# Forgetting attention's projections as seven products of quarters in place of eight, in a stage of eight heads

## The reference

```python
h = _rmsnorm(x, norm_w) * (1.0 + scale[:, None, :]) + shift[:, None, :]
proj = jnp.einsum("bsd,de->bse", h, w_in)
z_ssm, xbc, dt_raw, q, k, v, z_att, f_logit, g_logit = jnp.split(proj, offsets, axis=-1)
...
    logits = jnp.einsum("bhqd,bhkd->bhqk", qi, k).astype(jnp.float32) * scale
    logits = logits + fi[..., :, None] - f_cum[..., None, :]
    logits = jnp.where(pi[:, None] >= kpos[None, :], logits, -jnp.inf)
    probs = jax.nn.softmax(logits, axis=-1).astype(v.dtype)
    return jnp.einsum("bhqk,bhkd->bhqd", probs, v)
...
return o * jax.nn.silu(z)
```

## Time and profile before

| | us |
|---|---|
| median of 3 runs | 2056.05 |
| lowest and highest | 2053.98 to 2056.51 |
| the profiled execution | 2053.39 |
| its span, first to last instruction | 2051.7 |
| stage 5's eight heads in it | 626 to 1153 |

### The profile page before, as it was taken

The page is one execution under the profiler, slowest core; times in us unless marked ns, Lnnn a source line. Parts: engine busy times, 40 slices in busy tenths (PEclk is TensorE's granted clock), DMA queues, the critical chain, the costliest instruction groups (busy, mean ns, idle before and its releaser), DMA issues. The chain is left out here.

```text
span 2051.7 us, 26009 instructions
## 1 busy us (share of the span) xinstructions
PE 1942.3 (95%) x9700; PEld 1565.9 (76%) x9700; DVE 992.7 (48%) x1217; ACT 770.7 (38%) x1143; POOL 161.0 (8%) x319
## 2 busy tenths in 40 slices
PE   6899999999999999999999999969999998999997
PEld 4678787777887887888878788747777877888786
DVE  5586444555322334333343344479343344655865
ACT  4423343244213443444343342243234345442422
POOL 1000110110100000000000010002100001110100
PEclk8899999999999999999999999989999999999998
DMA  8541655543531111111112343232411111211302
GB/s 269 204 64 41 103 96 110 103 139 118 155 101 31 41 41 51 31 41 41 41 31 61 123 147 99 82 112 77 120 45 44 33 31 41 63 31 36 124 29 92
DMA packets 165535, 166.35 MB, mean 81 GB/s; under 512 B 10594, under 2 KB 143130, under 8 KB 165210
## 3 DMA queue, kind: packets, MB, share of 16 engines
q1 hardware_dynamic: 151424, 116.01, 18.3%
q0 software_dynamic: 13760, 49.30, 10.8%
q10 hardware_dynamic: 282, 0.09, 0.0%
HBM read 132.22 MB, written 33.16 MB: 81 GB/s over the span
## 5 line engine op out<-in xcount | busy, mean ns | idle before, releaser
L288 PE MATMUL acc<-ha_hi,w_hi 128*128 128x512 f32 x1152 | 469.1, 407 | 5.6 <-ACT stash L301 4.4
L288 PE MATMUL acc<-ha_hi,w_lo 128*128 128x512 f32 x1152 | 452.1, 392 | 0.0
L288 PE MATMUL acc<-ha_lo,w_hi 128*128 128x512 f32 x1152 | 450.6, 391 | 0.0
L288 PEld LDWEIGHTS acc<-ha_hi,w_hi 128*128 128x128 f32 x1152 | 217.7, 189 | 50.5 <-issue 6.5
L288 PEld LDWEIGHTS acc<-ha_hi,w_lo 128*128 128x128 f32 x1152 | 217.0, 188 | 47.7
L288 PEld LDWEIGHTS acc<-ha_lo,w_hi 128*128 128x128 f32 x1152 | 217.8, 189 | 42.0
L257 DVE TENSOR_TENSOR w_lo<-w_raw,w_hi 128x1024 fp32r<-128x1024 f32 x128 | 157.6, 1231 | 159.1 <-ACT w_hi L253 156.0
L271 PE MATMUL acc<-ha_hi,w_hi 128*128 128x512 f32 x592 | 187.3, 398 | 28.1 <-DVE ha_lo L1801 13.5
L271 PE MATMUL acc<-ha_lo,w_hi 128*128 128x512 f32 x592 | 184.5, 393 | 0.0
L271 PE MATMUL acc<-ha_hi,w_lo 128*128 128x512 f32 x592 | 183.9, 392 | 0.0
L271 PEld LDWEIGHTS acc<-ha_hi,w_hi 128*128 128x128 f32 x592 | 110.3, 190 | 58.8 <-issue 15.7
(11 more groups left out here) (444 smaller groups left out, 2749.1 us busy)
## 6 DMA issues: line engine op xcount, KB each, us to landing
w_raw<-in_w_in SPq DMA_DIRECT2D x99, 512.0 KB, 3.9
acs_bc<-acs_scr POOLq DMA_DIRECT2D x8, 1024.0 KB, 16.0
w_raw<-in_w_out SPq DMA_DIRECT2D x11, 512.0 KB, 3.9
x_tok<-in_x SPq DMA_DIRECT2D x8, 512.0 KB, 7.3
w_scale<-in_w_ada SPq DMA_DIRECT2D x8, 512.0 KB, 9.6
w_shift<-in_w_ada SPq DMA_DIRECT2D x8, 512.0 KB, 8.9
xt_scr<-xt SPq DMA_DIRECT2D x1, 4096.0 KB, 18.2
w_ada_g<-in_w_ada SPq DMA_DIRECT2D x8, 512.0 KB, 10.1
```

The source lines that it names most:

```text
L288: mm = pe.matmul(acc[:, 0, half * HALF:(half + 1) * HALF], w[:, n % 2, k, :], x[:, k, half * HALF:(half + 1) * HALF], start=(k == 0 and i ...
```

## The change

A pair of weight tiles (q and k of a head; v and z; two gate tiles) times the activations is a product of a matrix of 2 x 2 quarters with one of 2 x 2 quarters: the two tiles, each cut into rows 0 to 511 and 512 to 1023, and h cut in the same rows and into two halves of the tokens. That takes eight products of quarters, each of 4 k x 3 passes = 12 matmuls. The new kernel uses Strassen's form (in the variant of Winograd), which takes seven, with sums of quarters as operands and sums of the products as results:

- `a11`, `a12`, `s2`, `s1`, `s3`, `s4`, `a22` name the seven weights of a pair, in the order in which they run. Two pairs make a head: products 0 to 6 and 7 to 13.
- The sums of weights are made by VectorE for each pair: `weight_sums` (two operations and drains) and `weight_sums_in_place` (two more). Each of the 14 operands of 128x512 is then split in its own: `product_hi` on ScalarE, `product_lo` on VectorE. They rotate through four slots in the same buffers, which is why a loop body has two heads (`odd`).
- The sums of the quarters of h (`t1`, `t2`, `t3`, `t4`) are made once, ahead of the loop, by VectorE, and split as well; they and the other new buffers lie where `ya_hi` and `ya_lo` were.
- The product's result is read from PSUM not by ScalarE alone: `keep` (ScalarE, four a head) and `read` (VectorE, ten a head, with an addition), and `add_kept5` adds once more.
- A head's high and low part of y go to memory (`y_hi_scr`, `y_lo_scr`) and are loaded into `ya_hi` and `ya_lo` in the last head, by four DMAs, three of which stage 6 waits for ahead of its first matmul (`rows`).
- The order of each engine in a head is written out line by line. `fox_fills` and the sharing by parts are gone.
- The semaphores count products now, so later waits on them are shifted by `counted`.

```diff
+        PRODUCTS_EXTRA = (14 - 4) * FOX_HEADS
+        def counted(n):
+            return n + (PRODUCTS_EXTRA if n >= N_MIX2 else 0)
...
+        def product_lo(dve, q, h, odd):
+            dve.wait_ge(hi_done, FIRST + q + 1 + PER_HEAD * h)
+            dve.tensor_tensor(product_slot(w_lo, q, odd), weight_of(q), product_slot(w_hi, q, odd).bitcast(F32), ALU.subtract
+                              ).then_inc(lo_done, 1)
+        def weight_sums(dve, pair, h):
+            a11, a21, a22 = w_raw[:, W0, K1, :], w_raw[:, W1, K1, :], w_raw[:, W1, K2, :]
+            dve.drain()
+            raw_landed(dve, 0, pair, h)
+            raw_landed(dve, 1, pair, h)
+            dve.tensor_tensor(a21, a11, a21, ALU.subtract)
+            dve.drain()
+            dve.tensor_tensor(w_sum[:, :, :], a22, a21, ALU.subtract)
+            dve.drain().then_inc(w_summed, 1)
...
         def sp_5(sp):
+            product_done(9)
+            sp.wait_ge(y_saved, Y_SAVED + 48 * last)
+            sp.dma_start(ya_hi[:, 0:4, :].bitcast(F32), y_hi_scr[:, 0:4, :]).then_inc(y_back, 16)
+            product_done(10)
+            sp.dma_start(ya_hi[:, 4:7, :].bitcast(F32), y_hi_scr[:, 4:7, :]).then_inc(y_back, 16)
+            for i in range(2):
+                load_w(sp, N_MIX2 + i, cols(io["w_proj_att"], i * P))
+            product_done(11)
+            sp.dma_start(ya_lo[:, 0:4, :].bitcast(F32), y_lo_scr[:, 0:4, :]).then_inc(y_back, 16)
+            sp.wait_ge(*read_count(12, last))
+            sp.wait_ge(late_saved[0], LATE_SAVED)
+            sp.dma_start(ya_lo[:, 4:7, :].bitcast(F32), y_lo_scr[:, 4:7, :]).then_inc(y_tail, 16)
+            save_late(2, 12)
+            save_late(3, 13)
...
         def pe_5(pe):
+                def fill(q):
+                    pe.wait_ge(lo_done, FIRST + q + 1 + PER_HEAD * h)
+                    pe.wait_ge(*read_count(q - 2, h))
...
+                    for k in range(KH):
+                        for i, (w, x) in enumerate(((w_h, hi), (w_h, lo), (w_l, hi))):
+                            mm = pe.matmul(bank(q), w[:, k, :], x[:, k, :], start=(k == 0 and i == 0),
+                                           stop=(k == KH - 1 and i == 2))
...
+                scores(0)
+                scores(1)
+                fill(0)
+                fill(1)
+                scores(2)
+                fill(2)
+                fill(3)
+                turn_probs(0)
+                fill(4)
+                weigh_values(0)
...
         def act_5(act):
+                keep(0)
+                hi(3)
+                exps(0)
...
+                copies(5)
+                copies(6)
+                exps(7)
+                keep(10)
+                copies(7)
...
         def dve_5(dve):
+            split_lo(dve, N_FOX + 1)
+            quad(quad_12, K1, T2)
+            quad(quad_11, K1, T1)
+            dve.tensor_tensor(quad_11[:, :, :], quad_12[:, :, :], quad_11[:, :, :], ALU.subtract)
+            quad(quad_22, K2, T2)
+            dve.tensor_tensor(quad_12[:, :, :], quad_22[:, :, :], quad_12[:, :, :], ALU.subtract)
+            split_lo(dve, N_FOX + 2)
+            dve.tensor_tensor(quad_22[:, :, :], quad_22[:, :, :], quad_11[:, :, :], ALU.subtract)
+            t_lo(1, t1_lo[:, :, :], quad_11[:, :, :], t1_hi[:, :, :])
+            quad(quad_21, K2, T1)
+            dve.tensor_tensor(quad_21[:, :, :], quad_21[:, :, :], quad_22[:, :, :], ALU.subtract)
+            t_lo(2, t3_lo[:, :, :], quad_12[:, :, :], t3_hi[:, :, :])
+            t_lo(3, t2_lo[:, :, :], quad_22[:, :, :], t2_hi[:, :, :])
+            split_lo(dve, N_FOX + 3)
...
+                normalise(7)
+                read(11)
+                gate(0)
+                add_kept5(1)
+                read(12)
...
+                    weight_sums(dve, 2, h)
+                    lo(14)
+                gate(1)
...
+                    lo(15)
+                    weight_sums_in_place(dve)
+                read(13)
```

More of the change, by code:

```diff
@@ new lines, in head @@
+                copies(0)
+                exps(2)
+                keep(3)
+                copies(1)
+                copies(2)
+                hi(7)
+                hi(8)
+                hi(9)
+                exps(3)
+                exps(4)
+                copies(3)
+                hi(10)
+                hi(11)
+                keep(7)
+                exps(5)
+                copies(4)
+                hi(12)
+                exps(6)
+                hi(13)
+                copies(5)
@@ L1520, in head @@
+                copies(6)
+                exps(7)
+                keep(10)
+                copies(7)
+                if last:
+                    split_hi(act, N_MIX2)
+                else:
+                    hi(14)
+                    hi(15)
                 act.wait_ge(y_gated, 2 * h + 4)
                 if last:
-                    act.wait_ge(late_saved[0], LATE_SAVED)
-                act.activation(row(ya_hi, h), y_head[:, :], ACT.Copy).then_inc(x_hi_done, 1)
-            with act.Fori(0, FOX_HEADS - 1) as h:
-                head(h)
@@ L1527, in act_5 @@
-            head(FOX_HEADS - 1, last=True)
+                    act.activation(ya_hi[:, FOX_HEADS - 1, :], y_head[:, :], ACT.Copy).then_inc(x_hi_done, 1)
+                else:
+                    act.wait_ge(y_saved, Y_SAVED + 48 * h)
+                    for i in range(2):
+                        e = act.activation(y_hi[i][:, :], y_head[:, i * HALF:(i + 1) * HALF], ACT.Copy)
+                    e.then_inc(x_hi_done, 1)
+                    hi(16)
+            with act.Fori(0, FOX_HEADS // 2 - 1) as j:
+                head(2 * j, 0)
+                head(2 * j + 1, 1)
@@ new lines, in head @@
+                lo(3)
+                read(1)
+                normalise(0)
+                lo(4)
+                read(2)
+                lo(5)
+                lo(6)
+                normalise(1)
+                logits(2)
+                read(4)
+                normalise(2)
+                add_kept5(0)
+                logits(3)
+                read(5)
+                weight_sums(dve, 1, h)
+                lo(7)
+                logits(4)
+                lo(8)
+                normalise(3)
@@ new lines, in head @@
+                read(6)
+                lo(9)
+                normalise(4)
+                weight_sums_in_place(dve)
+                logits(5)
+                read(8)
+                lo(10)
+                normalise(5)
+                logits(6)
+                lo(11)
+                read(9)
+                normalise(6)
+                logits(7)
+                dve.drain().then_inc(fbc_used, 1)
+                lo(12)
+                lo(13)
+                normalise(7)
+                read(11)
@@ L1586, in dve_5 @@
+            with dve.Fori(0, FOX_HEADS // 2 - 1) as j:
+                head(2 * j, 0)
+                head(2 * j + 1, 1)
+            head(FOX_HEADS - 2, 0)
+            head(FOX_HEADS - 1, 1, last=True)
             end_stage(dve, 5)
```

366 lines of the change are left out of this document (271 added, 95 removed).

## The result

| | us |
|---|---|
| before, median of 4 runs | 2056.28 (2053.98 to 2058.67) |
| after, median of 4 runs | 2004.02 (2003.16 to 2004.76) |
| ratio, 95% interval | 0.9746 (0.9729 to 0.9762) |
| profiled execution, before and after | 2053.39 and 2004.76 |

The change takes 52.3 us by the medians, where 40 were forecast. The rest of this text works with the 48.6, which can be followed in the two traces.

A forecast was written before the change was run, and what follows sets the result against it. TensorE at its pace was taken to bound stage 5. Loop 43.6 less, minus 2.5 ahead and 1 behind, gave 40.1 us less: 2053.4 to 2013.3 profiled, 2016.0 as median; 8-in-10 range 2008 to 2038.

The forecast's parts named there:

- The removed matmuls: In each head, 24 fewer matmuls at 0.227 us save 5.44 us, 43.5 us over eight heads.
- The waits of `weigh_values`: In the heads, TensorE's waits for ScalarE's copy of the turned probabilities go, saving 4.9 us in all.
- one more change of kind: In each head, one more change between fills and attention on TensorE costs about 0.1 us, 0.8 us in all.
- The allowance for missed slack: In the heads, some tight places delay TensorE: 0.5 us a head, 4 us in all.
- VectorE's load: In a head, VectorE's busy time rises by 20.1 us to 44.9; with mask waits 48.8 of 60, so it fits.
- the rival: In the heads, VectorE's slack is not enough and TensorE waits 2 to 4 us a head: 2036 us; chance 20%.
- The slow rival: In the heads, VectorE becomes the bound at 66.1 us a head: about 2061 us, slower; chance 7%.
- Ahead of the loop: Before the first head, sums of h's quarters delay tile +3's low part; TensorE waits, costing 2.5 us.
- A lower granted clock in stage 5: In the attention stage, a listed sign that the forecast is wrong; no size given.
- Behind the loop: After the last product, returning y and the later `gate6` load together cost 1 us (bounds -0.6 and +11).
- The delay that I feared from GpSimd: After the last product, `gate6` loads later; VectorE's work moves some 4 us, leaving N_MIX2+2's low part no slack.
- GpSimd's copies under VectorE: In a head, q's copies slow VectorE's low parts by at most 0.8 us, hidden; 6.4 us in eight heads if uncovered.

The follow-up runs named there:

- The changed order alone: Kernel before with the last three parts of the fills (t = 5, 6, 7) moved between `turn_probs` and `weigh_values`: 2045.87 us, ratio 0.9954.
- the two runs with more work on it: Changed kernel with low parts of a head's product weights computed twice on VectorE: all 14, 2044.95 us; seven, 2012.93 us.
- the kernel with +3 early: Changed kernel with VectorE making tile +3's low part ahead of those of `t3` and `t2`: 2001.95 us, ratio 0.9738.
- two products twice: Changed kernel with the matmuls of products 3 and 10 of each head done twice, 24 more a head: 2049.37 us, ratio 0.9973.
- 172 operations: Kernel before with four heads in the body of VectorE's loop (two turns): 2055.38 us, one run.
- 43 and 86 operations: Kernel before, with one head in VectorE's loop body (median 2056.28 us), and with two heads in it (2056.49 us, one run).

## Why the prediction was too high

The time lies 12 us below the forecast and 4 below the low end of the range. The ledger holds 8.5 of the 12. The other 3.5 say nothing of the kernel: the forecast added 2.7 us to come from the profiled execution to the median, and after the change the profiled one lies 0.7 above its median. By the steps of the prediction:

**The removed matmuls: right.** 5.44 us a head were forecast and 5.45 measured.

**The waits of `weigh_values`: the mechanism right, the size wrong, and the largest miss.** I took the 4.9 us of the wait row as the gain of something to do in that place. The changed order alone gave 9.35 us, and the changed kernel is 1.4 us a head, 11 us, shorter than its matmuls explain. Of this the changed order alone gave 1.15 us a head, and 1.08 are seen in the starts at t = 6 and 7. The row is right in who waits for whom, but its idle starts at a modelled end, and for the price of a gap one must compare starts: 1.28 us from `turn_probs` to `weigh_values`, where seven transposes at 0.11 take 0.8. Both starts are in the trace of before. I also charged 0.8 us for one more change of kind; no run prices it by itself. Where the last 0.3 us of the 1.4 a head come from was not separated: the written order differs in more places than these, and the products are read in another way.

**The allowance for missed slack: half right in size, wrong in kind.** I put down 4 us since eight places had 0.3 to 1.5 us of slack. None was missed: the steady heads have no wait at all. The loss was 2.6 us where 4 stood in the sum, and it came from two jumps of VectorE's loop, which I had not considered, as the trace of before has seven jumps without any. Together, 43.6 + 11.2 - 2.6 = 52.2 us, and the ledger has 51.6.

**VectorE's load: right, and the rival rightly not the likeliest.** 43.5 us busy for 44.9. I had found it idle 7.7 us a head; the two runs with more work on it put what can be used at some 4. The rival's price was right in kind: with 9.8 us more of work a steady head grows by 3.9 to 4.7 us. The slow rival, heads of 66 us with VectorE as the bound, was 7 us a head away; even with the 9.8 us more the heads without a jump took 63.8 at most.

**Ahead of the loop: the wait right, the cost short by its second half.** The wait ahead of +3 was to be 2.5 us and is 2.43, for the reason given. But in the 4.6 us behind it the granted clock is 0.63, and pairs of matmuls start 0.85 us apart instead of 0.45: 1.9 us more, and none of it with the wait away. The upper bound of 4 was just passed (4.4). A lower granted clock in stage 5 was named as a sign of being wrong, and for this stretch it was one.

**Behind the loop: the transfer right, the price too high.** In the 20 us from 1086 on the DMA engines moved 333 GB/s and not 230. The transfers were to land 1.6 us behind the last product (the prediction's own numbers, 19.5 us for 6.8 million bytes and 2 to start, less 20.9, give 0.6); N_MIX2 starts 1.3 us behind it (1106.81 + 0.23 to 1108.37), released by them. So the wait of N_MIX2 for a DMA, named as a sign of being wrong, is there with 1.2 us, but shorter than the 2.1 us of before; and in the run with VectorE's loop written out ScalarE holds it for 1.0 us instead. Against before that is 0.9 us less, where 0.6 less was forecast for this part. The delay that I feared from GpSimd did happen: timelines of GpSimd and VectorE after, for the earlier trace rows,

```profile
1115.59 0.55 POOL L2020 DMA_DIRECT2D gate<-ga_scr  x1 [23.99 <-DMA ga_scr<-next_z]
```

```profile
1128.19 1.22 DVE L265 TENSOR_TENSOR w_lo<-w_raw,w_hi 128x1024 fp32r<-128x1024 f32 x1
```

`gate6` is loaded 7.2 us behind N_MIX2's start instead of 2.7. The low part that is queued behind it ends at 1129.4, needed at 1108.37 + 21.8 = 1130.2: 0.8 us of slack are left of 4, and no time is lost. So the term was -0.9 and not +1.

**GpSimd's copies under VectorE.** In the kernel with +3 early, the first sum of weights falls under them and takes 1.46 us instead of 0.69 (618.85 and 620.39 above), as the low part in the earlier trace rows took 2.07 for 1.23. In the heads of the changed kernel two low parts under the copies take 1.85 us where such a pair takes 1.29 elsewhere (677.09 and 624.81), and VectorE waits 1.5 us for ScalarE behind them. The Trainium skill (SBUF — State Buffer, "SBUF: two separate sides") has the rule that fits; as forecast it cost the sum nothing.

**The range.** Its low end of 2008 was to allow for no stall and nothing behind the loop; by its own terms that would be 2016 - 4 - 1 = 2011. What went past it is the order term, 11.2 us where 4.9 - 0.8 = 4.1 stood in the sum. It had been given no end of its own: the 4.9 stood as a fixed number, though the row behind it was an idle time and not a difference of starts. Against it stand the 1.9 us of the clock, which no bound held either.

## What to carry to other kernels

Price a wait that is to go by the difference of two starts, with and without work in that place, and not by the idle time that is listed before it. Where a long body is made for a loop, look at each jump back: an engine with time to spare hides it, and the same engine, once it is loaded, does not. And a wait of about 2 us of a busy TensorE can cost nearly as much again in clock: one line moved in VectorE's order shortened its stretch by 4.3 us, for a wait of 2.4. It does not always, as the last part shows.

## What the runs showed of the hardware

- **Jumps of VectorE.** At the jump back of a body of 154 operations VectorE stood idle 2.67 and 2.90 us (2.47 to 2.90 with the traces of two products twice and of +3 early, which have the same body), with 172 operations 2.02 us; with 43 and 86 operations no idle is seen. TensorE and ScalarE show no idle of this kind over 0.3 us in the same stage, TensorE with over 600 matmuls in its body.
- **Clock behind a wait.** After TensorE had stood 1.93, 2.43 and 3.58 us in otherwise full work, the matmuls that followed were granted 0.50 to 0.63 of the full clock for 3 to 4 us (6 after another wait of 3.54), that is for the most part the lower of its two levels (1.2 for 2.4 GHz). After waits of 1.16 to 1.66 us it stayed at 1.00. A head with the wait of 1.93 us was 3.5 us longer than its neighbours. In between it can go either way. The wait ahead of N_MIX2 is the same in the kernel before and in the one with the order changed, 2.06 and 2.07 us, and it left the clock at 1.00 in the first and not in the second. The windows behind it, before and then order changed:

```profile
1155.52:1158.00 2.48, 2.48 (x11) 2.07 (x12) 1.17 (x1) 1.01 (x1) 0.00 (x0) 1.00 1.01 276
```

```profile
1147.74:1150.00 2.26, 2.26 (x6) 1.78 (x7) 1.18 (x1) 0.78 (x1) 0.00 (x0) 0.51 1.00 268
```

- **A pace without change.** 168 matmuls in products of 12, each with other weights and another bank, keep the pace of fills of one tile: with 192 matmuls a head they take 64.51 us, and the kernel before with its order changed takes 64.76.
